# Gated pieces added to X by VectorE alone, none by POOL

## The reference

```python
def _ffn_half(s, mod, g, wg, wu, wd):
    shift, scale, gate = mod
    h = _modulate(_rmsnorm(s, g), shift, scale)
    return s + 0.5 * gate * _swiglu(h, wg, wu, wd)
...
        x = x + lat_m[5] * y          # y: the mixer's result
```

## Time and profile before

| | |
|---|---|
| runs | 2620.45, 2625.8, 2617.8 us; median 2620.45 |
| profiled execution | 2627.55 us, span 2625.8 us |
| PE busy | 2505.7 us (95%), mean granted clock 0.986 |
| DVE busy | 1724.6 us (66%), of it L1673 655.2 and L1687 545.5 |
| ACT busy | 1092.5 us (42%) |
| POOL busy | 446.0 us (17%), of it L2156 83.0 in 48 additions, mean 1736 ns |
| chain that ended last | PE 62%, DVE 3%, ACT 2%, POOL 1% |

### The profile page before, as it was taken

The page is one execution under the profiler, slowest core; times in us unless marked ns, Lnnn a source line. Parts: engine busy times, 40 slices in busy tenths (PEclk is TensorE's granted clock), DMA queues, the critical chain, the costliest instruction groups (busy, mean ns, idle before and its releaser), DMA issues.

```text
span 2625.8 us, 35204 instructions
## 1 busy us (share of the span) xinstructions
PE 2505.7 (95%) x13498; PEld 2094.4 (80%) x13498; DVE 1724.6 (66%) x2514; ACT 1092.5 (42%) x1876; POOL 446.0 (17%) x462
## 2 busy tenths in 40 slices
PE   4999999999999999999989999999999999999998
PEld 3678987779979878877648888888888888777997
DVE  6967876857995766776865564675565655345454
ACT  3466544556554212236644322324322224334543
POOL 1101111001111111114831112111112110000111
PEclk9999999989999999999989999999999999999999
DMA  8654885536783554542102343442343443221452
GB/s 306 214 176 169 289 290 209 189 135 209 243 279 111 187 176 152 189 157 73 65 16 81 114 175 113 161 176 99 119 178 111 169 168 113 96 74 65 159 197 95
DMA packets 118294, 413.02 MB, mean 157 GB/s; under 512 B 13552, under 2 KB 17776, under 8 KB 118128
## 3 DMA queue, kind: packets, MB, share of 16 engines
q1 hardware_dynamic: 117568, 409.06, 44.6%
q10 hardware_dynamic: 560, 1.72, 0.2%
HBM read 409.68 MB, written 1.05 MB: 156 GB/s over the span
## 4 chain that ended last, share of the span: by engine, by line
PE 62%; DVE 3%; ACT 2%; POOL 1%; issue 1%; DVEq 0%; POOLq 0%; ACTq 0%
PE ps L1102 18%; PE ps L1104 18%; PE ps L1103 18%; PE ps L1318 2%; PE ps L1295 1%; PE ps L1255 1%; PE ps L1286 1%; DVE sl L1673 1%; PE ps L1266 1%; POOL ap L2195 1%; POOL X L2156 1%; ACT F L1440 1%; DVE F L1790 1%; DVE mjunk L1687 0%; ACT sh L1381 0%
## 5 line engine op out<-in xcount | busy, mean ns | idle before, releaser
L1102 PE MATMUL ps<-hH,sh 128*128 128x256 f32 (+1 forms) x2560 | 844.2, 330 | 6.2 <-DVE hL L1761 3.5
L1103 PE MATMUL ps<-hL,sh 128*128 128x256 f32 (+1 forms) x2560 | 837.6, 327 | 0.0
L1104 PE MATMUL ps<-hH,sl 128*128 128x256 f32 (+1 forms) x2560 | 837.6, 327 | 0.0
L1673 DVE TENSOR_TENSOR sl<-raw,sh 128x1024 fp32r<-128x1024 f32 x534 | 655.2, 1251 | 123.4 <-ACT sh L1381 122.7
L1381 ACT ACTIVATE sh<-raw 128x1024 fp32r<-128x1024 f32 x534 | 540.2, 1039 | 394.6 <-PE ps L1104 322.2
L1687 DVE CUSTOM_DVE_ANT_0 mjunk<-raw,cB,V 128x1024 bf16<-128x1024 f32 x384 | 545.5, 1420 | 30.7 <-DMA C<-in_cst 8.4
L1102 PEld LDWEIGHTS ps<-hH,sh 128*128 128x128 f32 x2560 | 481.6, 188 | 58.3 <-issue 7.3
L1103 PEld LDWEIGHTS ps<-hL,sh 128*128 128x128 f32 x2560 | 483.0, 189 | 48.9 <-issue 1.7
L1104 PEld LDWEIGHTS ps<-hH,sl 128*128 128x128 f32 x2560 | 481.6, 188 | 48.3
L2168 POOL TENSOR_TENSOR uLl<-F,uHh 128x256 fp32r<-128x256 f32 (+1 forms) x132 | 166.5, 1261 | 989.9 <-ACT uHh L1562 854.2
L1102 PE MATMUL ps<-sh,uHh 128*128 128x512 f32 x792 | 316.7, 400 | 15.3 <-DVE sl L1673 15.3
(11 more groups left out here) (169 smaller groups left out, 2256.0 us busy)
## 6 DMA issues: line engine op xcount, KB each, us to landing
raw<-in_w SPq DMA_DIRECT2D x756, 512.0 KB, 4.4
raw<-in_w SPq DMA_DIRECT2D x16, 256.0 KB, 3.8
cB<-in_rpb SPq DMA_DIRECT2D x64, 64.0 KB, 2.5
X<-in_x ACTq DMA_DIRECT2D x1, 1024.0 KB, 11.7
X<-in_ctx SPq DMA_DIRECT2D x1, 1024.0 KB, 7.9
out<-X SPq DMA_DIRECT2D x2, 512.0 KB, 2.6
raw<-in_w SPq DMA_DIRECT2D x2, 288.0 KB, 6.1
cB<-in_c ACTq DMA_DIRECT2D x1, 512.0 KB, 5.6
```

What stands on the lines that cost most here:

```text
L1102: self.e.matmul(out, lh, rh, start=start, stop=False)
L1103: self.e.matmul(out, lh, rl, start=False, stop=False)
L1104: return self.e.matmul(out, ll, rh, start=False, stop=stop)
L1673: self.e.tensor_tensor(lo[:, 0:w], raw[:, 0:w], hi[:, 0:w].bitcast(F32), ALU.subtract).then_inc(self.sems["w_lo"], 1)
```

## The change

`gated` loses `fast`: VectorE makes the addition behind every gating, and POOL's part of the step is gone. It touches all 68 gated pieces, in the feed-forwards and in the two mixers' output projections; 20 of them were VectorE's already. Nothing else in the list of steps is moved.

```diff
@@ Plan @@
-    def gated(self, t, half, b, gid, fast):
+    def gated(self, t, half, b, gid):
...
-                self.gated(t, half, b, gid, fh == 1 and half == 1)
+                self.gated(t, half, b, gid)
...
-            self.gated(t, half, b, gid, half == 1)
+            self.gated(t, half, b, gid)
@@ Vector.gated @@
-        if s["fast"]:
-            x = self.m["X"][:, t, half * 512:(half + 1) * 512]
-            self.wait_ge(self.got("gf", f))
-            self.x_ready(s["x0"])
-            self.e.tensor_tensor(x, x, F, ALU.add).then_inc(self.sems["v_sb"], 1)
-            self.done("v_sb", ("left", f), s["x1"])
+        x = self.m["X"][:, t, half * 512:(half + 1) * 512]
+        self.wait_ge(self.got("gf", f))
+        self.x_ready(s["x0"])
+        self.e.tensor_tensor(x, x, F, ALU.add).then_inc(self.sems["v_sb"], 1)
+        self.done("v_sb", ("left", f), s["x1"])
@@ Pool @@
-    def gated(self, s):
-        if s["fast"]:
-            return
-        t, half, f = s["t"], s["half"], s["f"]
-        x = self.m["X"][:, t, half * 512:(half + 1) * 512]
-        self.wait_ge(self.got("gf", f))
-        self.x_ready(s["x0"])
-        self.e.tensor_tensor(x, x, self.buf(f)[:, :], ALU.add).then_inc(self.sems["p_sb"], 1)
-        self.done("p_sb", ("left", f), s["x1"])
```

More of the change, by code:

```diff
@@ L351, in gated @@
         self.x_at[(t, half)] += 1
-        self.add("gated", t=t, half=half, b=b, f=f, gid=gid, s=t // 2, fast=fast, x0=x0, x1=self.xs(t, half))
+        self.add("gated", t=t, half=half, b=b, f=f, gid=gid, s=t // 2, x0=x0, x1=self.xs(t, half))
         self.left(b)
@@ L2111, in __init__ @@
         self.parts = dict(start=self.start, sq=self.sq, rs=self.rs_pow,
-                          gated=self.gated, pout=self.pout, glu1_c=self.glu1_c,
+                          pout=self.pout, glu1_c=self.glu1_c,
                           glu2_b=self.glu2_b, pads=self.pads, tap_p=self.tap_p, ln_out=self.ln_out)
```

## The result

The changed kernel took 2616.78 us (median of 20 runs, 2608.59 to 2621.57). Twenty runs of the kernel before had a median of 2624.74 us. The ratio is 0.9971, with a 95% interval from 0.9963 to 0.9979. That is 8.0 us less, 0.30%, with the interval reaching from 5.5 to 9.7 us. The profiled execution has a span of 2615.1 us.

What follows compares the result with a forecast made beforehand. TensorE, busy 95% of the span, bounds the kernel, waiting most for `sl`. Resumptions −5.7, clock −0.8 and −1.5 sum to −8.0 us: from the median 2620.45 to 2612.4 us, range 2606 to 2619.

Steps and rivals of the forecast that it cites:

- What bounds it: At B and D VectorE idles 2.91 and 5.34 us for ScalarE's copies, behind squares that wait for POOL's additions.
- What it removes: 48 POOL additions, 83.0 us of POOL's time, and their collisions that stretch VectorE's instructions, 2.4 us at C.
- The price of a pair: On VectorE, gating plus addition takes 1.33 us against 0.60 for a gating: 0.73 a piece, 2.9 for four.
- The burst: VectorE's queue from t0 to the needed `sl`: 12.66 us at A and B, 11.52 at C and D.
- TensorE's resumptions: Changes of −0.2 us at A, −2.3 at B, +0.5 at C, −3.7 at D; sum −5.7.
- The clock: Less time at TensorE's low 1.2 GHz level behind the waits: −0.8 us at B, −1.5 at D, A and C unchanged.
- Rival 1: The clock falls behind C and D as well: −4.9 us, 2615.6; chance 0.15.
- Rival 2: The clock does not fall behind waits of 2.3 us at A and B: −11.2 us, 2609.3; chance 0.14.
- rival 3: VectorE's stretch at A to D stays, not being POOL's doing: +5.0 us, 2625.4; chance 0.05.
- Rival 4: The convolution's own waits eat B's gain, so only A, C and D count: −4.9 us, 2615.6; chance 0.09.
- The edits at nothing: The other 32 additions cost nothing; no new `sl` wait at 1391, 1964, 2148, 2405, 2512 or 2602.
- A to D: Layer 0 feed-forward bursts, t0 their first gating: A, C first hidden half; B, D second; waits 2.49, 4.57, 0.68, 4.85 us.

Runs made afterwards that it cites:

- sq_later: Kernel before, POOL still adding, but the square of a tile's first 512 columns is taken ahead of the gating of its second 512; 2612.48 us, ratio 0.9962.
- vec_first: Kernel before, with VectorE adding in the first hidden half and all second 512 columns, POOL still adding pieces that are squared; 2622.36 us, ratio 1.000.
- pool_idle: Changed kernel, with POOL also making 48 additions of a constant tile that nobody reads; 2627.81 us, ratio 1.0023 of the kernel before.
- jobs_later: Changed kernel, with both modulation jobs moved behind the first and second finished tile of the second 512 columns; 2610.45 us, ratio 0.9939 of the kernel before.

## Why the prediction was right

The predicted saving was 8.0 us and the measured one is 8.0. The mechanism held; that the two figures agree to the last digit is luck, since the terms came to −7.1 and 1.2 us that the prediction had no term for made up the rest (below). The saving lies at the bound of 0.3%, as the prediction said. The predicted time, 2612.4 us, is 4.4 below the measured 2616.78, in the range: the difference was taken from a median of three runs, 2620.45, that was 4.3 us under the median of twenty.

**What bounds it.** Held. B and D waited for ScalarE's copies behind squares that waited for POOL; `sq_later` freed them without the change, and `vec_first` left them as they were with the rest of the change made.

**What it removes.** Held for the stretch. VectorE's busy time grew by 20.4 us (the page of before has 1724.6) though 48 additions at 0.69 us, 33.2 us, were put on it; the remaining 12.8 us came back from its other instructions. `pool_idle` brought the stretch back with additions of no use. The Trainium skill (SBUF — State Buffer, "SBUF: two separate sides") has a GpSimd operation that reads SBUF and a VectorE operation with two SBUF inputs exclude each other for a whole instruction. The trace agrees roughly for the `mjunk` of `pool_idle`: it starts at 959.41, POOL's last operation ends at 955.94 + 4.44 = 960.38, 0.97 us later, and the `mjunk` is 0.78 us longer. The recorded lengths do not bear it out for VectorE's additions there, which have two SBUF inputs as well: 0.69 to 0.81 us each beside POOL's three in 4.44 us, which alone would be 3.8 (3 x 1.26) with no room for 2.3 us of additions between them. Either the rule is too strict for them or a recorded length holds more than the time in which an operation keeps the other out; the records don't tell which.

**The price of a pair.** 1.33 us, as worked out from one row of another place.

**The burst.** This is the term that was mis-sized, and the fault is in the prediction's 2 x 2.53 for two jobs. The needed pieces started at t0 + 12.89 and 12.88 (A, B) and 11.75 (C, D), against 12.66 and 11.52. All the 0.23 us are in the two modulation jobs: from the first `mjunk` to the `sl` behind the last 964.77 − 959.47 = 5.30 us, not 2 x 2.53. The row used, 940.74 to 943.27, is of a job with an `sl` piece behind it. A job with another job behind it takes 962.23 − 959.47 = 2.76.

**TensorE's resumptions.** The waits are 2.52, 2.53, 1.39 and 1.39 us against 2.3, 2.3, 1.2 and 1.2. The changes are A +0.04, B −2.05, C +0.71, D −3.46 us (start after less start before), −4.8 in place of −5.7. C was the loss that the prediction gave it, by 0.2 more.

**The clock.** At half speed for 2 x (1 − 0.69) x 5.5 = 3.4 us behind A, 2 x (1 − 0.73) x 6.3 = 3.4 behind B, none behind C and D. B regains 0.8 and D 1.5, as predicted. Rival 1 (a fall behind C and D) is out: behind waits of 1.39 us the clock stayed at 1.00. Rival 2 was not put to the test. It said that 2.3 us would not pull the clock down; the waits came out at 2.52 and 2.53, above the 2.49 that had pulled it down before. So −0.8 at B came right with a wait that the prediction had not forecast, and that is luck. `jobs_later` has waits a little below 2 us, and there the clock did both: 1.00 behind 1.95 us, 0.79 behind 1.93 us. What 2.3 us would have done stays open.

**The sum by the traces.** −4.8 − 2.3 = −7.1 us. From A's t0 to the end it is −8.25; the distances between the places show where: A to B +0.10, B to C −3.46, C to D +0.71, D to the end −5.60. B's own terms are −2.05 − 0.8 = −2.9, D's −3.46 − 1.5 = −5.0. So 1.2 us lie behind B and behind D in later stages, 0.6 each. Set matmul against matmul, D's lead over before is 4.9 us at 1785 and 5.4 at 2396, and the step between lies in 10 us of the attention, the same 41 matmuls before and then after:

```profile
2386.22:2395.74 9.52, 8.15 (x41) 7.33 (x42) 5.71 (x15) 5.48 (x13) 0.00 (x0) 0.66 0.00 0
...
2376.48:2385.26 8.78, 7.81 (x41) 7.18 (x42) 4.63 (x14) 4.79 (x13) 0.00 (x0) 0.61 0.00 1
```

There TensorE runs at the low clock for a part of the time in both kernels, but not for the same matmuls, and a wait of 1.06 us became 0.60. B's 0.6 us come in small steps along the convolution. No term of the prediction stands for any of it.

**Rivals 3 and 4.** The stretch went, so rival 3 fell. `pool_idle` shows what a stretch costs: 6.0 us more than the kernel before (2627.81 against 2621.82), where rival 3 said 5.0. The agreement means little: the prediction put 2 us of stretch a burst at 8.0 us in all (4 x 2.0), and 1.9 to 2.0 us a burst cost 14 (6.0 and the change's 8.0), since the clock fell for longer behind A and B, and behind C and D as well. Rival 4, a convolution that eats B's gain, fell: B to C is shorter by all of it.

**The edits at nothing.** Held at layer 1's feed-forward, the tightest (40.00 of 40.00 us busy again). The one additional wait for `sl` in the list (12 for 11) is at none of the six places named; where the two lists differ in number is at 700 to 733 us, ahead of A.

## What to carry to other kernels

A vector addition that is cheap in itself can cost what queues behind its result: follow the reader of the result and what stands behind that reader in its own queue, here ScalarE's weight copies behind squares of X. Before moving work to another engine, look whether the order on the waiting engine can be changed: putting the square later gave as much as the change. Taking one job that nobody there awaited out of the burst gave more than the change even with POOL adding (0.9942 against 0.9971 of the kernel before, the intervals apart). Look also at what else such a move shifts: here it drew the weights forward by a unit. A job that is moved away should land where nothing behind it is awaited; the second one landed ahead of the next norm and brought two new waits of 1.9 us. And a total that comes out right does not show that its terms did.

## What was not expected of the hardware

- Two modulation jobs in a row cost 0.23 us more than twice one with a low-part piece behind it: `mjunk` to `mjunk` 1.32 us within a job, 1.44 from job to job (960.79 to 962.23), behind the read of the sum.
- VectorE's additions of 512 columns took 0.69 to 0.81 us beside POOL's, while a `mjunk` of 1024 columns took 2.06 in place of 1.28. By these lengths the collision does not have one price for all operations; over a burst it was 1.9 to 2.0 us.
- In the six profiles in which VectorE has made the same 236 low parts ahead of A's t0, with nothing ahead of it changed, that t0 lies between 950.5 and 954.3 us. (In the five with jobs moved, where the order changes just ahead of it, it lies between 948.9 and 956.5.) The spans of before and after differ by 10.7 us, of which 2.5 arise there. The saving between medians, and the stretch counted from A's t0, are free of that.
- At A to D of the two kernels, waits of TensorE of 0.68 and 1.39 us were followed by a granted clock of 1.00, and those of 2.49 us and more by 0.59 to 0.73 over the next 5 to 6 us. In between the length of the wait alone does not tell: in `jobs_later` 1.95 us behind B left the clock at 1.00, and 1.93 us behind D was followed by 0.79 over 8.0 us.
